# A streaming encoder step: the prompt tokens' down projection as seven block products, with the up products in another order

## The reference

```
u  = x @ w_up                        # 1024 -> 2 x 2816 columns ("a" and "b")
c  = causal depthwise conv of width 3 over u, with bias
g  = silu(c_a) * c_b                 # 2816 columns
x  = LayerNorm(ALPHA * x + g @ w_down)   # 2816 -> 1024
```

## Time and profile before

| | |
|---|---|
| time, median of 3 runs | 2938.72 us (2938.63 to 2946.72) |
| span of the profiled execution | 2935.9 us; no other time of that execution is given |
| PE busy in the span | 2810.2 us (96%) |
| DVE, ACT, POOL busy | 1955.7, 1100.3, 1081.8 us |
| mean granted clock of PE | 0.984 |

### The profile page before, as it was taken

The page is one execution under the profiler, slowest core; times in us unless marked ns, Lnnn a source line. Parts: engine busy times, 40 slices in busy tenths (PEclk is TensorE's granted clock), DMA queues, the critical chain, the costliest instruction groups (busy, mean ns, idle before and its releaser), DMA issues. The chain is left out here.

```text
span 2935.9 us, 47457 instructions
## 1 busy us (share of the span) xinstructions
PE 2810.2 (96%) x16927; PEld 2491.0 (85%) x16927; DVE 1955.7 (67%) x3408; ACT 1100.3 (37%) x2112; POOL 1081.8 (37%) x858
## 2 busy tenths in 40 slices
PE   8898799999999999999999898998999999999997
PEld 7455578887899999998887898997899999998886
DVE  3466654566578888888556464445478888888556
ACT  5334542334353334332113464334354334332112
POOL 1254321112136666652226001112137666653224
PEclk9999899999999999999999999999999999999999
DMA  3100450113212112124223011113212212124222
GB/s 117 51 8 13 127 186 19 37 41 112 87 65 82 73 69 81 67 91 177 91 91 118 31 37 42 40 35 115 87 65 82 75 67 81 67 92 177 91 91 102
DMA packets 90614, 233.61 MB, mean 80 GB/s; under 512 B 21514, under 2 KB 35995, under 8 KB 89428
## 3 DMA queue, kind: packets, MB, share of 16 engines
q1 hardware_dynamic: 90484, 231.85, 22.6%
HBM read 181.97 MB, written 50.50 MB: 79 GB/s over the span
## 5 line engine op out<-in xcount | busy, mean ns | idle before, releaser
L136 PE MATMUL psum<-xT_hi,tk_w 128*128 128x320 f32 (+1 forms) x1536 | 453.6, 295 | 2.8 <-ACT tk_u L2582 2.8
L138 PE MATMUL psum<-xT_hi,tk_w 128*128 128x320 f32 (+1 forms) x1536 | 453.7, 295 | 0.0
L137 PE MATMUL psum<-xT_lo,tk_w 128*128 128x320 f32 (+1 forms) x1536 | 452.5, 295 | 0.0
L2304 POOL TENSOR_TENSOR tk_w<-tk_sums,tk_w 128x512 fp32r<-128x512 f32 x160 | 307.2, 1937 | 170.2 <-ACT tk_w L2602 170.2
L136 PEld LDWEIGHTS psum<-xT_hi,tk_w 128*128 128x128 f32 x1536 | 289.4, 188 | 3.1 <-issue 3.1
L137 PEld LDWEIGHTS psum<-xT_lo,tk_w 128*128 128x128 f32 x1536 | 289.6, 189 | 0.0
L138 PEld LDWEIGHTS psum<-xT_hi,tk_w 128*128 128x128 f32 x1536 | 288.9, 188 | 0.0
L136 PE MATMUL psum<-tk_t,tk_w 128*128 128x256 f32 x960 | 284.4, 296 | 3.3 <-POOL tk_w L2304 3.3
L138 PE MATMUL psum<-tk_t,tk_w 128*128 128x256 f32 x960 | 284.4, 296 | 0.0
L137 PE MATMUL psum<-tk_t,tk_w 128*128 128x256 f32 x960 | 283.7, 295 | 0.0
L3001 DVE TENSOR_TENSOR x_or_mix<-x_or_mix,psum 128x512 f32<-128x512 f32 x288 | 195.6, 686 | 131.4 <-PE psum L138 130.6
(11 more groups left out here) (462 smaller groups left out, 7067.4 us busy)
## 6 DMA issues: line engine op xcount, KB each, us to landing
tk_wraw<-in_w_up SPq DMA_DIRECT2D x88, 512.0 KB, 4.2
ates_between_projections<-tk_g SPq DMA_DIRECT2D x44, 576.0 KB, 2.8
tk_graw<-ates_between_projections SPq DMA_DIRECT2D x44, 576.0 KB, 6.1
tk_draw<-in_w_down SPq DMA_DIRECT2D x44, 512.0 KB, 5.4
x_between_sublayers<-x_or_mix SPq DMA_DIRECT2D x18, 512.0 KB, 2.6
tk_resid<-x_between_sublayers SPq DMA_DIRECT2D x18, 512.0 KB, 7.2
s_ckv<-in_c_ckv SPq DMA_DIRECT2D x8, 1024.0 KB, 6.3
retw_raw<-in_w_ret SPq DMA_DIRECT2D x32, 256.0 KB, 3.3
```

The lines of the kernel that those rows point to most:

```text
L136: nc.tensor.matmul(out, a[0], b[0], start=first, stop=False)
L137: nc.tensor.matmul(out, a[0], b[1], start=False, stop=False)
L138: return nc.tensor.matmul(out, a[1], b[0], start=False, stop=last)
L2304: nc.gpsimd.tensor_tensor(W7[:, i, 1], src, W7[:, i, 0].bitcast(F), ALU.subtract).then_inc(wl, 1)
```

## The change

**Down.** The prompt's product becomes a 2x2 block product: two groups of 4 token tiles by even and odd g blocks, by two halves of 512 columns. It is made with seven products (M1 to M7) in the order M2, M5, M3, M1, M6, M7, M4, once over the first 6 pairs of blocks and once over the other 5. A step (g, i, k) is one pair in one product: 4 tiles of 128 tokens, three matmuls of 512 columns each, and in M2, M5, M3 and M1 a fifth tile, which is the sample tokens' plain product. There are 77 steps in a layer. The products stay in PSUM over the 6 or 5 steps; M3, M6, M7 and M4 are summed onto the banks of the product ahead of them once DVE has taken that one out. Operands lie in 6 places, and the place of a step is filled again (ACT `g_hi`, `d_hi`; DVE `d_sum`, `g_lo`; POOL `d_lo`) when that step is over. The last product is made tile by tile (`last_tile`), and the norms follow in the order sample, 0, 1, ... 7.

**Gates.** The sums of g that the products need are made beside `gate`, in odd windows over two blocks, and lie in HBM in another layout. An odd window stores 512 + 512 + 576 + 64 KB in four transfers, an even one 256 KB.

**Up.** The products come in the order A11, S2, A12, S3, S1, A22, S4; A12 and S4 are summed in PSUM; ACT takes the first result (`take_11`), and DVE needs 10 instructions of twice the size. Window 2 makes the weight sums of window 3 inside it.

```diff
+    GROUPS = (range(0, 6), range(6, NJ // 2))
...
+    wx = [m.at(f"{tag}operands{k}", PLACES[k], [P, 2, 2, 512], R) for k in range(6)]
...
+    M2, M5, M3, M1, M6, M7, M4 = range(7)
+    WITH_SAMPLE = (M2, M5, M3, M1)
+    ONTO = (M3, M6, M7, M4)
+    STEPS = [(g, i, k) for g in range(2) for i in range(7) for k in range(len(GROUPS[g]))]
...
+    def turn(g, i, x):
+        return 15 * g + (0 if i == M2 else 5 if i in (M5, M3) else 10) + x
...
-    A11, A12, S2, S3, A22, S1, S4 = range(7)
-    PRODUCTS = ((A11, X11), (A12, X21), (S2, T2x), (S3, T3x), (A22, T4x), (S1, T1x), (S4, X22))
+    A11, S2, A12, S3, S1, A22, S4 = range(7)
+    PRODUCTS = ((A11, X11), (S2, T2x), (A12, X21), (S3, T3x), (S1, T1x), (A22, T4x), (S4, X22))
+    BANK_OF = (0, 2, 0, 4, 6, 2, 6)
...
-            store_g(0)
-            store_g(1)
+            store_even(0, 0)
+            store_odd(1, 0)
             next_raw(2)
...
+            with sp.Fori(0, LOOP // 2) as r:
+                next_raw(2 * r + 3)
+                store_even(2 * r + 2, r + 1)
+                next_raw(2 * r + 4)
+                store_odd(2 * r + 3, r + 1)
...
+            def load_d(g, k):
+                pair = GROUPS[g][k]
+                for odd in range(2):
+                    sp.dma_start(draw_row(k, odd), A["w_down"][layer, 2 * pair + odd].rearrange("p (h n) -> p h n", h=2)).then_inc(dld[k], 16)
...
+            def load_g(n):
+                g, i, k = STEPS[n]
+                at, wide = G_AT[i]
+                if n >= 6:
+                    sp.wait_ge(al, n - 5)
+                sp.dma_start(graw[n % 6][:, 0:wide], A["g_mid"][layer][GROUPS[g][k]][:, at:at + wide]).then_inc(gld[n % 6], 16)
...
+            def d_lo(n):
+                g, i, k = STEPS[n]
+                pool.wait_ge(bh, n + 1)
+                nc.gpsimd.tensor_tensor(wx[k][:, 1, 1, :], d_operand(g, i, k), wx[k][:, 1, 0, :].bitcast(F), ALU.subtract).then_inc(bl, 1)
...
                 for i, (s, x) in enumerate(PRODUCTS):
                     pe.wait_ge(wl, 7 * jj + s + 1)
...
+                        bank = BANK_OF[i] + p
+                        if i == 2:
+                            pe.wait_ge(ea, 2 * jj + p + 1)
+                        elif i == 6:
+                            pe.wait_ge(ev, 5 * jj + 3)
+                        elif i == 5:
+                            pe.wait_ge(ev, 5 * jj + 1)
+                        elif first:
+                            pe.wait_ge(ur, min(13 + bank, 16))
+                        elif i == 0:
+                            pe.wait_ge(e11, jj)
                         else:
-                            pe.wait_ge(ev, 14 * jj + FREED[q])
+                            pe.wait_ge(ev, 5 * jj + {1: -1, 3: -3, 4: 0}[i])
...
+            def bank_free(g, i, x):
+                n = turn(g, i, x)
+                if i in ONTO:
+                    if x < 4:
+                        pe.wait_ge(ad, TAKEN[g, i - 1, x])
...
+            def down_step(n):
+                g, i, k = STEPS[n]
+                operands(n)
+                for x in range(tiles_of(i)):
+                    if k == 0:
+                        bank_free(g, i, x)
+                    if x == 4 and i == M5:
+                        pe.wait_ge(b2l, GROUPS[g][k] + 1)
+                    last = step_part(n, x)
+                    if ends_product(n):
+                        last.then_inc(dm, 1)
+                if not ends_product(n):
+                    last.then_inc(ds, 1)
+            def last_tile(x):
+                bank_free(1, M4, x)
+                for n in range(LAST_PRODUCT, len(STEPS)):
+                    if x == 0:
+                        operands(n)
+                    last = step_part(n, x)
+                last.then_inc(dm, 1)
...
+            for n in range(LAST_PRODUCT):
+                down_step(n)
+            for x in range(4):
+                last_tile(x)
+                if more and x == 2:
+                    f_t(0)
             if more:
+                for n in range(1, 5):
+                    f_t(n)
+                pe.wait_ge(fxlo, 2)
+                project_next(range(4))
                 f_t(5)
-                project_next(range(4))
+                project_next(range(4, KD))
                 f_t(6)
-                project_next(range(4, KD))
                 f_t(7)
...
+            def copy_g(j, odd, p):
+                act.wait_ge(gd, j + 1)
+                sample = cv[:, 0, US:].rearrange("p (b t) -> p b t", b=NB)[:, :, 2:]
+                to = gf[:, 1152 if odd else 512:1280 if odd else 640].rearrange("p (b t) -> p b t", b=NB)
+                if not odd:
+                    ge(act, ste, 32 * p)
+                    nc.scalar.activation(gf[:].rearrange("p (h n) -> p h n", h=2)[:, :, 0:512], cv[:, 0, 2:2 + SEQ].rearrange("p (h n) -> p h n", h=2), ACT.Copy)
+                nc.scalar.activation(to, sample, ACT.Copy).then_inc(gc, 1)
+            def take_11(j):
+                act.wait_ge(pr, 14 * (j - STD) + 6)
+                act.wait_ge(cvd, 2 * j)
+                act.wait_ge(sk, 2 * j)
+                nc.scalar.activation(both_u(0, 0), both(PS[:, 0:2, 0:256]), ACT.Copy)
+                nc.scalar.activation(sample_u(0, 0), as_sample(PS[:, 1, :]), ACT.Copy).then_inc(e11, 1)
...
+            def window(j, odd, p):
                 keep_s1(j, 0)
                 keep_s1(j, 1)
                 silu(j - 1)
...
+                copy_g(j - 1, 1 - odd, p if odd else p - 1)
+                take_11(j)
+            def whole_window(j, odd, p):
+                window(j, odd, p)
+                for i in range(6):
                     w_hi(j + 1, i)
...
+                centre_tap(j, 1, odd, p)
+                w_hi(j + 1, S4)
+                centre_tap(j, 0, odd, p)
...
+            def gate(j, odd):
+                a, b = cv[:, 0], cv[:, 1]
                 dve.wait_ge(si, j + 1)
                 dve.wait_ge(cvd, 2 * j + 2)
...
+                nc.vector.tensor_tensor(a[:, 2:], a[:, 2:], b[:, 2:], ALU.mult).then_inc(gd, 1)
+                dve.wait_ge(gd, j + 1)
+                if odd:
+                    dve.wait_ge(gc, j)
+                    nc.vector.tensor_tensor(gf[:, 640:1152], gf[:, 640:1152], a[:, 514:2 + SEQ], ALU.add).then_inc(gch, 1)
+                    dve.wait_ge(gch, j)
+                    nc.vector.tensor_tensor(b[:, 514:2 + SEQ], gf[:, 640:1152], gf[:, 0:512], ALU.subtract).then_inc(gch, 1)
+                    dve.wait_ge(gch, j + 1)
+                    nc.vector.tensor_tensor(b[:, 2:514], a[:, 2:514], b[:, 514:2 + SEQ], ALU.subtract).then_inc(gr, 1)
+                else:
+                    nc.vector.tensor_tensor(b[:, 2:514], a[:, 2:514], a[:, 514:2 + SEQ], ALU.subtract).then_inc(gr, 1)
...
+            def from_s1(j):
+                dve.wait_ge(pr, 14 * (j - STD) + 4)
+                dve.wait_ge(ea, 2 * (j - STD) + 2)
+                dve.wait_ge(sk, 2 * j)
+                nc.vector.tensor_tensor(both_u(0, 1), both(s1[:, :, 0:256]), both(PS[:, 2:4, 0:256]), ALU.add)
+                nc.vector.tensor_tensor(sample_u(0, 1), as_sample(s1[:, 1, :]), as_sample(PS[:, 3, :]), ALU.add).then_inc(ev, 1)
+            def plus(j, n, bank, out, x):
                 jj = j - STD
...
+                dve.wait_ge(pr, 14 * jj + 2 * n + 2)
+                nc.vector.tensor_tensor(both_u(*out), both_u(*x), both(PS[:, bank:bank + 2, 0:256]), ALU.add)
+                nc.vector.tensor_tensor(sample_u(*out), sample_u(*x), as_sample(PS[:, bank + 1, :]), ALU.add).then_inc(ev, 1)
             def window(j, nxt=True):
...
+                from_s1(j)
                 if nxt:
                     w_sum(j + 1, 0)
-                take_u3(j, 0)
+                dve.wait_ge(ev, 5 * (j - STD) + 1)
+                plus(j, 3, 4, (1, 0), (0, 1))
                 if nxt:
                     w_sum(j + 1, 1)
-                take_u3(j, 1)
-                if nxt:
                     w_sum(j + 1, 2)
-                take_21(j, 0)
+                dve.wait_ge(ev, 5 * (j - STD) + 2)
+                plus(j, 4, 6, (1, 1), (1, 0))
                 if nxt:
                     w_sum(j + 1, 3)
-                take_21(j, 1)
...
+            def take_12(j):
+                plus(j, 6, 6, (0, 1), (0, 1))
+            def window_end(j, odd):
                 conv(j, 1, 1)
-                take_12(j, 1)
+                take_12(j)
                 conv(j, 1, 0)
                 conv(j, 0, 1)
                 conv(j, 0, 0)
-                gate(j)
+                gate(j, odd)
...
+            conv(1, 1, 1)
+            conv(1, 1, 0)
             t_lo(3, T1x, t1[:])
-            window(2, False)
-            take_p5(2)
-            for n in range(4):
-                w_sum(3, n)
-            window_end(2)
...
+            conv(1, 0, 1)
+            conv(1, 0, 0)
+            gate(1, 1)
+            window(2)
+            window_end(2, 0)
...
+            def g_lo(n):
+                g, i, k = STEPS[n]
+                dve.wait_ge(ah, n + 1)
```

(80 more changed lines are left out.)

776 lines of the change are left out of this document (405 added, 371 removed).

## The result

The changed kernel takes 2973.68 us in the median of 4 runs (2971.17 to 2975.35), the kernel before 2940.13 (2938.63 to 2946.72) on the same chip: ratio 1.0106, 95% interval 1.0087 to 1.0124. It is slower by 33.5 us. Forecast were 2918 us and 2896 to 2945. The profiled execution has a span of 2969.4 us and took 2971.17.

A forecast was written before the change was run, and what follows sets the result against it. The prediction took PE's own list to set the time, except at the joints. Its terms, -59.9 + 1.6 + 15.7 + 4 + 9 + 9 = -20.6 from 2935.9, gave 2915.3, with 2.8 carried over 2918 us; range 2896 to 2945.

The forecast's parts named there:

- Matmuls, -59.9: Down stages: 132 fewer matmuls a layer at an unchanged pace of 0.227 us, -59.9 us over 2 layers.
- Rival 4: Down matmuls: the count falls but not the time, a pace slower than 0.227 in unlooped code; 2967 at 0.25; chance 0.03.
- The up loop, +4: Up loop: 0.2 us lost in each of 20 odd windows, the gate chain having one microsecond of room; bounds 0 and +20.
- Rival 2: Odd up windows: gate chain comes late, 20 us for each us past the room; 2954 with 2 us each; chance 0.11.
- Window 2, +15.7: Window 2, up: S2 waits 1.5 us, S4 8.3 behind late weights; both layers together +15.7, bounds +9 and +26.
- Down, inside, +1.6: Within down stages: stalls of 4.1 us a layer instead of 4.0 and 2.6, +1.6 us; bounds -6.6 to +14.
- The first take at 24.4: a stall of 1.9 us: Down start: DVE's first take of M2 24.4 us behind the last up product, stalling PE at M5's fourth tile 1.9 us.
- The tails, +9 and +9: Ends of both layers' down stages: DVE's list delays the last product and bounds the end, +9 us in each layer.
- PE stalls 4 us, 8 where POOL's `scale` (2.4 us each) blocks: Ahead of the last product: PE waits for DVE's last g_lo in M7, 4 us, or 8 if POOL blocks DVE.
- Rival 3: Down steps: bound by DVE and POOL excluding each other, 3.1 against 2.72 us a 4-tile step; 26 us, 2944; chance 0.09.

The follow-up runs named there:

- e3: Changed kernel with SyncE's loads of window 3's weights ahead of the stores of the first odd tile; its median falls by 17.0 us.
- e5: Changed kernel with GpSimd's low parts of the down weights replaced by zeros (memset), so their correction product is not computed: 2936.5 us.
- e2: Changed kernel with statistics, roots and scalings of the second to fifth row tile moved behind the last but one product; layer 1 292.1 against 293.0 us.
- e8: Changed kernel with the second to fifth row tile's norms behind the last but one product, done by VectorE alone; layer 1 292.2 against 293.0 us.
- e11: Changed kernel with the second round's block differences for M7 and M4 one product earlier in VectorE's list; median falls by 4.0 us.
- e13: Changed kernel with row-tile half statistics taken early, in M6 and ahead of the last product's takes; median falls by 2.7 us.
- e15: Changed kernel with GpSimd's down-weight low parts zeroed (correction product not computed) and window 3's weight loads ahead of the stores: 2915.4 us.

## Why the prediction was wrong

- **Matmuls, -59.9: right.** Stage time less stalls and slow pitch (in layer 0 also less 0.8 us of a transposed tile) is 240.0 us in each layer for 1056 matmuls, 0.227 each. Rival 4 is out.
- **The up loop, +4: nothing.** PE is busy 423.3 of 423.3 us in layer 0 and 423.4 of 423.4 in layer 1. e3 puts the whole stage within 1.3 us of before in layer 0 and 5.0 in layer 1, where its waits lie in window 2. Rival 2 did not happen.
- **Window 2, +15.7: the mechanism right, the size short.** S4 waited 8.1 and 9.6 us (forecast 8.3), and e3 shows that the place of `next_raw(2)` does it. But the stages lost 26.8: A12's wait of 1.8 was not foreseen, layer 1 waited longer, and about 3 us a layer went by as slow matmuls behind these stalls.
- **Down, inside, +1.6: the step that failed first.** "The first take at 24.4: a stall of 1.9 us" let DVE wait for g data and counted its rests and sums at 0.68 each. DVE hardly waited (busy 32.96 of 33.1), and e4 issued the g loads ahead of the stores without effect. The list was lengthened by GpSimd's low parts, 0.68 to 1.75 and 0.28 to 1.34, and the take began 32.3 us behind the stage's first matmul. The stall was 8.8. To it came 2.8 a layer at the end of M5 in the second round, where I had 0.7. In all some 14.5 us of stalls a layer up to M7's end, against the 4.1 of the forecast.
- **The tails, +9 and +9: the mechanism right, mis-sized by half.** From the last product's ideal start (M7's end) and 13.6 us, it is 34.0 us to the end in layer 1 (11.2 of stall, 2.8 of slow matmuls, 20.0 behind the last) and 45.9 to the next phase in layer 0, where 16.6 and 25.6 were before: +17 and +20. I had the list, with "PE stalls 4 us, 8 where POOL's `scale` (2.4 us each) blocks"; it was 11.1, and 5.0 without GpSimd's rests (e5). The 20 us behind the last matmul stay without them (20.2). That DVE's work is what ends the tail, as the prediction had it, is shown by e2 and e8 (PE freed, layer 1's end under 1 us sooner) against e11 and e13 (DVE relieved, its end 3.8 and 4.5 us sooner).
- **A term that was missing: matmuls at half pace behind a stall.** Over the four stages it is (6.7 - 0.8) + (6.8 - 0.2) in the down stages and, estimated as what the losses of the up stages exceed their stalls, 3.0 + 3.3 there: 18.8 us. Each of the long stalls had to be priced with it.
- **Rival 3, 0.09, was the true cause in the wrong place.** I rejected it because takes read PSUM and places lie 10 us ahead. Both hold in steady steps, where PE does not wait. The exclusion told where DVE's list had no air: the start of the stage and M7. Its price was 37 us and not 26, and 2918 + 37 = 2955 lies outside the range.

Without GpSimd's reading rests and without window 2's late loads (e15) the kernel takes 2915.4. The forecast's 2918 had contained the second and not the first, so the agreement is partly chance. What stays open is how the 37 us split between DVE's own time and the slow matmuls that follow each stall; no run holds the one and changes the other. Nor does a run take away the rest of GpSimd's work in the tail, so what the exclusion adds to the 20 us behind the last matmul is not measured.

## What to carry to other kernels

When a change moves sums from TensorE to VectorE, add up VectorE's list at its lengthened durations wherever GpSimd reads SBUF beside it, and ask stage by stage whether the list still has air; the worst places are joints, where two stages' work overlap. Where several waits hang on one engine's list, moving one instruction up uncovers the next: price the list's sum, and treat freeing TensorE as worth nothing until the engine behind it has been shown to have time. Loads for the next window go ahead of stores that nobody waits for: one line here was worth 17 us.
